# Five attentions of a one-core kernel: the product with V is issued ahead of the turning of the next probabilities

## The reference

```python
# first block, 8 heads over 2 key heads, two branches (all keys of the selected blocks, and a window)
s = einsum('bgrqd,bgqkd->bgrqk', q, k) + bias      # 512 queries x 512 keys, causal
p = softmax(where(dist >= 0, s, NEG_INF))
o = einsum('bgrqk,bgqkd->bgrqd', p, v)             # added to the output with a gate
...
# second block, in each of its two layers
logits = einsum('bqhcd,bshcd->bchqs', q, k) * scale   # difference attention: 4 heads x 2 parts, values 128 wide
attn = p[:, 0] - lam * p[:, 1];  out_b = attn @ v
logits = einsum('bqhd,bqkhd->bhqk', q, k_sel) * scale # sparse attention: 8 heads, 128 keys picked for each query
out_a = softmax(logits) @ v_sel
```

## Time and profile before

| | |
|---|---|
| median of 3 runs | 3427.3 us (3427.09 to 3433.63) |
| the profiled execution, its own time | 3441.54 us |
| its span in the profile | 3439.8 us |
| PE / DVE / ACT / POOL busy | 92% / 52% / 36% / 8% |
| mean granted clock of TensorE | 0.958 |
| the five attentions begin (first scores) | 296.8, 978.1, 1037.4, 1681.4, 1745.3 us |

### The profile page before, as it was taken

The page is one execution under the profiler, slowest core; times in us unless marked ns, Lnnn a source line. Parts: engine busy times, 40 slices in busy tenths (PEclk is TensorE's granted clock), DMA queues, the critical chain, the costliest instruction groups (busy, mean ns, idle before and its releaser), DMA issues. The chain is left out here.

```text
span 3439.8 us, 40721 instructions
## 1 busy us (share of the span) xinstructions
PE 3154.7 (92%) x15574; PEld 2629.1 (76%) x15574; DVE 1788.7 (52%) x2623; ACT 1241.3 (36%) x1702; POOL 258.0 (8%) x237
## 2 busy tenths in 40 slices
PE   5848899999988999999879999999899989799997
PEld 4627788788877888888777888878777889688886
DVE  3255476735885533357865333385446364453333
ACT  2124443324355322234463222356344534232221
POOL 0001000000400000004000000001000172000000
PEclk8968999999999999999999999999999989899998
DMA  3210232222212332222123332233133301323321
GB/s 107 65 61 13 74 98 98 86 94 79 86 27 74 98 93 94 94 92 82 37 60 100 98 97 87 85 117 105 63 121 141 126 29 50 122 86 98 98 98 49
DMA packets 182273, 290.76 MB, mean 85 GB/s; under 512 B 12093, under 2 KB 113040, under 8 KB 181609
## 3 DMA queue, kind: packets, MB, share of 16 engines
q1 hardware_dynamic: 182121, 288.71, 25.8%
HBM read 268.61 MB, written 10.60 MB: 81 GB/s over the span
## 5 line engine op out<-in xcount | busy, mean ns | idle before, releaser
L624 DVE TENSOR_TENSOR w_lo<-ring,w_hi 128x2048 fp32r<-128x2048 f32 (+1 forms) x209 | 477.6, 2285 | 585.7 <-ACT w_hi L618 585.4
L343 PE MATMUL psum<-h_hi,w_hi 128*128 128x512 f32 x1824 | 716.8, 393 | 2.4 <-SPq L126 1.5
L345 PE MATMUL psum<-h_hi,w_lo 128*128 128x512 f32 x1824 | 710.0, 389 | 0.0
L344 PE MATMUL psum<-h_lo,w_hi 128*128 128x512 f32 x1824 | 709.9, 389 | 0.0
L618 ACT ACTIVATE w_hi<-ring 128x2048 fp32r<-128x2048 f32 (+1 forms) x209 | 396.2, 1896 | 635.3 <-PE psum L345 624.5
L343 PE MATMUL psum<-s_hi,w_hi 128*128 128x512 f32 x1088 | 435.3, 400 | 53.3 <-DVE w_lo L624 29.9
L345 PE MATMUL psum<-s_hi,w_lo 128*128 128x512 f32 x1088 | 431.6, 397 | 0.0
L344 PE MATMUL psum<-s_lo,w_hi 128*128 128x512 f32 x1088 | 429.9, 395 | 0.0
L343 PEld LDWEIGHTS psum<-h_hi,w_hi 128*128 128x128 f32 x1824 | 342.4, 188 | 82.4 <-issue 10.3
L344 PEld LDWEIGHTS psum<-h_lo,w_hi 128*128 128x128 f32 x1824 | 342.4, 188 | 72.8 <-issue 2.4
L345 PEld LDWEIGHTS psum<-h_hi,w_lo 128*128 128x128 f32 x1824 | 342.3, 188 | 71.6
(11 more groups left out here) (433 smaller groups left out, 3919.4 us busy)
## 6 DMA issues: line engine op xcount, KB each, us to landing
ring<-in_w_in SPq DMA_DIRECT2D x66, 1024.0 KB, 5.1
ring<-in_w_up SPq DMA_DIRECT2D x44, 1024.0 KB, 5.2
ring<-in_w_down SPq DMA_DIRECT2D x33, 1024.0 KB, 4.9
ring<-in_w_gate SPq DMA_DIRECT2D x22, 1024.0 KB, 5.3
ring<-in_w_ffn_in SPq DMA_DIRECT2D x22, 1024.0 KB, 5.1
ring<-in_w_out SPq DMA_DIRECT2D x16, 1024.0 KB, 5.1
ring<-in_w_ffn_down SPq DMA_DIRECT2D x11, 1024.0 KB, 4.9
second_k_hi<-second_k_hi SPq DMA_DIRECT2D x32, 128.0 KB, 2.2
```

The costliest lines, as they stand in the source:

```text
L343: nc.tensor.matmul(bank, l_hi, r_hi, start=start, stop=False)
L344: nc.tensor.matmul(bank, l_hi, r_lo, start=False, stop=False)
L345: return nc.tensor.matmul(bank, l_lo, r_hi, start=False, stop=stop)
L624: self.core.nc.vector.tensor_tensor(lo, self.core.raw(s, a)[:, :, 0:n], hi.bitcast(F32), ALU.subtract).then_inc(r.split[s], 1)
```

## The change

In both functions the block of PE's list that turns the probabilities of step n - 2 is moved behind the block that multiplies those of step n - 3 with V. Nothing else differs: the same instructions, waits, banks and buffers, and the lists of the other engines are the same. In `attend_layer` the `split` stays at the end of the iteration, now behind the turning.

```diff
--- before.py
+++ after.py
@@ -1517,14 +1517,6 @@
                     q = q_of(u)[:, t * P:(t + 1) * P]
                     nc.tensor.matmul(core.bank(n % DEPTH)[:, 0:nk], q, k_hi, start=True, stop=False)
                     nc.tensor.matmul(core.bank(n % DEPTH)[:, 0:nk], q, k_lo, start=False, stop=True).then_inc(scored, 1)
-                if 2 <= n < steps + 2:
-                    s = n - 2
-                    pe.wait_ge(exp_done, s + 1)
-                    if s >= DEPTH:
-                        stored(pe, s - DEPTH)
-                    for k in range(0, keys(s), P):
-                        mm = nc.tensor.transpose(core.bank(3 + s % DEPTH)[:, k:k + P], pb[:, s % DEPTH, k:k + P], ident)
-                    mm.then_inc(turned, 1)
                 if n >= 3:
                     s = n - 3
                     u, t, g = s // TT, s % TT, s // per_bank
@@ -1539,6 +1531,14 @@
                                               pt[:, s % DEPTH, c * P:(c + 1) * P], v_of(u, c, columns),
                                               start=(c == 0), stop=(c == t))
                     mm.then_inc(weighed, 1)
+                if 2 <= n < steps + 2:
+                    s = n - 2
+                    pe.wait_ge(exp_done, s + 1)
+                    if s >= DEPTH:
+                        stored(pe, s - DEPTH)
+                    for k in range(0, keys(s), P):
+                        mm = nc.tensor.transpose(core.bank(3 + s % DEPTH)[:, k:k + P], pb[:, s % DEPTH, k:k + P], ident)
+                    mm.then_inc(turned, 1)
 
         @block.vector
         def _(dve):
@@ -1700,14 +1700,6 @@
                     nc.tensor.matmul(core.bank(n % DEPTH)[:, 0:nk], q, k_hi[:, u, 0:nk], start=True, stop=False)
                     nc.tensor.matmul(core.bank(n % DEPTH)[:, 0:nk], q, k_lo[:, u, 0:nk], start=False, stop=True
                                      ).then_inc(scored, 1)
-                if 2 <= n < steps + 2:
-                    s = n - 2
-                    pe.wait_ge(exp_done, s + 1)
-                    if s >= 2:
-                        stored(pe, s - 2)
-                    for k in range(0, keys(s), P):
-                        mm = nc.tensor.transpose(core.bank(3 + s % 2)[:, k:k + P], pb[:, s % DEPTH, k:k + P], ident)
-                    mm.then_inc(turned, 1)
                 if n >= 3:
                     s = n - 3
                     u, t, g = s // TT, s % TT, s // per_bank
@@ -1723,6 +1715,14 @@
                                               pt[:, s % DEPTH, c * P:(c + 1) * P], v_of(u, c, columns),
                                               start=(c == 0), stop=(c == t))
                     mm.then_inc(weighed, 1)
+                if 2 <= n < steps + 2:
+                    s = n - 2
+                    pe.wait_ge(exp_done, s + 1)
+                    if s >= 2:
+                        stored(pe, s - 2)
+                    for k in range(0, keys(s), P):
+                        mm = nc.tensor.transpose(core.bank(3 + s % 2)[:, k:k + P], pb[:, s % DEPTH, k:k + P], ident)
+                    mm.then_inc(turned, 1)
                 if split_after(n):
                     split(split_after(n))
```

## The result

Beside runs of the kernel before, the changed kernel took 3488.02 us (median of four, 3483.14 to 3496.3) against 3430.47 (four, 3427.09 to 3446.87). The ratio is 1.0161, 95% interval 1.0135 to 1.0186: slower by 1.6%, about 55 us (46 to 64); the medians differ by 57.6. The forecast was 3478, in a range from 3452 to 3500.

The account below looks back on a forecast made before the run. PE, busy 92% of the span, was taken as the bound, with DVE setting the pace beside the picking. Terms 25 + 8.4 + 18 = 51.4 us on 3427.3 gave 3478; range 3452 to 3500.

Parts of the forecast that it names:

- each copy now lies in series: Between turning and product, copies no longer fit; stalls of 0.37, 0.32 and 0.51 us for 256, 384 and 512 keys.
- The size in the first attention: 15 full units of four steps at 1.53 us, about 0.4 in the first unit, end +1.5: sum 25 us.
- the cover: PE's work between a turning and its product: 0.67, 0.46, 0.73 and 0.92 us for 128, 256, 384 and 512 keys.
- The refill: A product that waited fills PE anew, costing 0.11 us a stall, bounded by 0 and 0.11; 0.33 per unit.
- The ends: At a stage's end no scores cover a copy: +1.5 us in first and sparse attention, 1.4 in difference attention.
- Difference attention: Two stages: nothing in the first 24 steps, then 2.8 us for steps 24 to 31 and 1.4 at the end, 4.2 each.
- Sparse attention: Two stages at 9.0 us each: 4.0 for 5 units, 0.4 the first, 3.1 two units without splits, 1.5 the end.
- 0.8 a unit: Sparse attention units with splits: 384-key stall with refill 0.43 us, ACT free 0.35 late; between 0.4 and 1.2.
- the rival of the clock: Clock at 1.2 GHz in half of the first attention: 38 us on top, 3515; chance 0.05.
- Half the price: The waits hide each other, so the next copy starts at once: about 25 us, 3452; chance 0.10.
- No change: Stages not bound by PE's order, or PE takes the turning ahead of the waiting product: 3427; chance 0.05.
- Faster: `finish` comes earlier, so DVE gets its banks sooner in difference attention: at most 13 us, 3414; chance 0.04.

Follow-up runs that it names:

- experiment 2: Product taken four steps back instead of three: on the changed kernel 3436.75 against 3439.8, ratio 0.9993; on the kernel before 3432.08, ratio 0.9975.
- experiment 4: Changed kernel with ACT also copying the first attention's 512-key tiles: unit 6.56 to 6.45 us, total 3489.74 against 3438.23, ratio 1.0157.
- experiment 3: Kernel before with only some turnings moved, in `attend` alone: 128 keys, 3438.22, ratio 0.9999; 128 and 256 keys, 3444.16, ratio 1.0009.
- experiment 5: Later picking rounds shortened to 32 columns: on the kernel before 3424.32, ratio 0.9963; on the changed kernel 3483.61, ratio 1.0147.
- experiments 1: Kernel before with the move in `attend` alone: 3469.89 against 3439.8, ratio 1.0088; in `attend_layer` alone: 3462.99, ratio 1.0067.

## Why the prediction was right, and where its terms were off

*That each copy now lies in series.* Shown. The chains were put at 0.62, 0.83, 1.05 and 1.43 and measured 0.63, 0.84, 1.06 and 1.38; 48 waits stand in the first attention where about 45 were foreseen; giving the distance back removes the loss (experiment 2), and changing only the copy's length moves the unit by as much (experiment 4).

*The size in the first attention* was low by 5 us: a unit grew by 1.86 (4.70 to 6.56), where 1.53 was summed. The term that was mis-sized is the cover, "the turning's slot and the next scores' slot". It was read from the old order, where a product stands behind the turning. In the new order the scores stand there, and the covers of the three larger tiles are 0.14 + 0.25, 0.25 + 0.32 and 0.35 + 0.44, 1.75 together (experiment 2) where 0.46 + 0.73 + 0.92 = 2.11 was taken. That is 0.36 more of stall. Some 0.25 of it is the neighbour; the other 0.11 is the hidden wait of experiment 2, which the rows held (0.38 for 0.32, 0.49 for 0.44), and which "nothing in it waits" had passed over. The 128-key tile, held to be free, stalls 0.04 (experiment 3), the chain of 512 keys was 0.05 shorter (its turning's 0.66 held the refill of the same wait), and the other two 0.01 longer each. So the stalls come to 1.20 + 0.36 + 0.04 - 0.03 = 1.57; read off the two timelines, after against the new order unstalled, the scores' slots grow by 0.04, 0.46, 0.50 and 0.58, which is 1.58. Where the saved turning slots went, the products' slots show: they grew by as much, and a chain in series doesn't get that back.

*The refill, 0.11 a stall.* Right in size: the products' slots of 0.33, 0.55, 0.77 and 1.00 are 0.06, 0.10, 0.10 and 0.11 above those of the run without waits, 0.37 a unit against 0.33. Stalls and refills, 1.95, are counted from 4.60, not 4.70, since the hidden wait cost the kernel before 0.1 a unit in a list that the prediction called "full". 4.60 + 1.95 = 6.55.

*The ends.* +1.5 foreseen, +1.83 measured in the first attention: from its last scores matmul of 512 keys to the last product it took 4.85 us before and 6.68 after. The covers of its first tiles are short by the same error. The 0.4 put for the first unit isn't there (its first scores matmul of 512 keys came 1.33 and 1.32 us behind the stage's start), but the distance to the next one grew by 2.04 (5.80 to 7.84).

*Difference attention.* 4.2 foreseen, 4.8 and 4.6 measured. Beside the picking the units stayed at 7.10, so the cost of nothing that was put there held but for the first two, and experiment 5 shows both that the picking is the cover and what it is worth. In layer one the units of the last 8 steps grew by 0.56 (6.54 to 7.10) and 1.75 (4.70 to 6.45), 2.3 for 2.8, the first two distances together by 0.65 where nothing was put, and the end by 1.8 for 1.4.

*Sparse attention.* 9.0 foreseen, 6.9 and 6.8 measured; the term "0.8 a unit" for the units with a split was too high. In layer one the distances between 512-key scores went from 6.34, 6.36, 6.36, 7.73, 5.58, 5.76 and 4.70 to 7.26, 6.89, 6.89, 7.97, 6.56, 6.55 and 6.55. Where ACT squares for the difference attention, a unit was held by ACT and DVE at 6.36 already, PE had idle time in it, and it grew by 0.53; the one of 7.73 grew by 0.24; behind them the growth was 0.98, 0.79 and 1.85. The lateness of ACT is there, but only beside the squares. From the timeline of the sparse attention in the changed kernel, with a square (line 2524) and the rounding ahead of the copy:

```profile
1094.05 0.61 ACT L2524 ACTIVATE work<-normed 128x512 f32<-128x512 f32 x1
...
1094.57 0.57 ACT L1771 ACTIVATE second_q<-psum 64x512 fp32r<-64x512 f32 x1
...
1095.05 0.46 ACT L1659 COPY work<-psum 128x384 f32<-128x384 f32 x1
...
1095.56 0.94 PE L1714 MATMUL psum<-work 128*128 128x128 f32 x6 [0.78 <-ACT work L1659]
```

This product waits 0.78, where behind a rounding without a square the same wait is 0.33 (at 1109.98), as in the first attention. So ACT behind a rounding alone is in time, which the prediction gave as its lower end, 0.4 a unit. Such a unit grew by 0.98 all the same (5.58 to 6.56, from 1066.28 before and 1106.60 after). Its scores' slots grew by 0.05, 0.01, 0.49 and 0.16 over the copies of 128, 256, 384 and 512 keys, 0.71 together: the split covers the copy of 256 keys, but the stall at 384 is 0.49 where 0.32 was summed, and 0.16 is left at 512. The products' slots grew by 0.47 and the turnings' shrank by 0.21, neighbours and refills together. So the lateness of ACT was put too high and the stalls too low. The splits do fill waits, as foreseen: a unit with splits took 5.58 and one without 4.70, and now both take 6.55. Summed, the first five distances grew by 3.2 where 4.4 was put, the last two by 2.6 for 3.1, and the end by 1.8 for 1.5. The rest of the difference to 9.0 is the start: in the profiled execution before, the first scores matmul of 512 keys came 2.14 us behind the stage's start, in the one after 1.36, with nothing edited ahead of it. That is 0.8 of the 2.1, and not of the change's making: in the traces of experiments 1, 3 and 5 with the old order there it is anything from 1.35 to 2.16.

*The sum* came out right, 51.4 against 53.0 by stages and 55 by the runs, in part by luck: the first attention was 5 low, the two sparse ones were 4 high together. The arithmetic of the sparse attention doesn't deserve credit for it. Two slips changed nothing: there are 192 turnings (480 transposes), not 320, and the rival of the clock comes to 3516 (3427.3 + 51.4 + 37.6), not 3515.

*The rivals.* Half the price: a unit grew by more than the full price, and each of its three longer products waits (48 waits in 16 units). The clock: the granted clock reads 1.00 in every window of the changed kernel above, with PE idle 1.05 of 6.56 us, in three pieces for the most part; over the whole span it is 0.958 before and 0.96 after. The Trainium skill ("TensorE: Matmul & The Clock Gate", A second HAM failure mode: psum-queue depth-cycling) tells of a bf16 kernel whose clock swung with short idle stretches between groups of matmuls. The trace of this kernel doesn't show that. No change: PE did not let a turning pass a waiting product; every turning in the timeline starts behind it. Faster: DVE's pace beside the picking is 7.10 with either order, so an earlier product gave it nothing.

Left open: why the 0.1 lies in the product's slot when a turning follows, and in the turning's when a product follows. The runs show only that it moves. What makes the start of the sparse attention differ between executions is open too.

## What to carry to other kernels

In a queue that runs in order, a group that waits for another engine's answer needs the whole round trip as work between it and the instruction that asked; before two groups change places, compare that round trip with what will then lie between, tile by tile. Read the cover from a stretch in which the same neighbours stand beside each other: here each turning's slot shrank by about 0.1 us for another neighbour, which was some 0.25 of the 0.36 us by which the covers were off. Check too that the stretch is free of waits: a group that starts 0.06 behind what it needs has waited, though the profile calls the engine busy; that was the other 0.11. If a distance is short, try a lag of one more step before any reordering: it cost no buffer here and gave 0.25%, though in the first attention by easing waits other than the one in view.

## What the runs showed of the hardware

- A group's slot depends on what follows it. A turning of 128 keys costs PE's list 0.11 us ahead of a product and 0.02 to 0.03 ahead of scores; a product of 128 keys costs 0.27 ahead of a turning and 0.15 ahead of scores.
- A product that starts after a wait takes 0.06 to 0.11 us more of PE's list than one that doesn't, whether it has two matmuls or eight; a turning of 512 keys that waited for its exponential took 0.66 instead of 0.60.
- Idle time in brackets understates a stall: 0.29, 0.33 and 0.42 stand for stalls of 0.46, 0.50 and 0.58, and the stall of 0.04 has none, nor has the 0.06 that the turning of 512 keys waited in the kernel before.
- PE was idle 16% of each unit, mostly in pieces of 0.3 to 0.4 us, through a stage of 107.6 us, and the granted clock stayed at 1.00.
